# Latent stage of a hybrid encoder layer: weighing in two halves, queries and folds at the weighing, rests of latent tiles on GpSimd

## The reference

```python
qh = jnp.einsum('bsr,re->bse', _rmsnorm(cq, mla_q_norm_g), w_q_up).reshape(B, S, H_MLA, MLA_NOPE + MLA_ROPE)
...
s = (jnp.einsum('bqhd,bkhd->bhqk', qnb, kn, preferred_element_type=jnp.float32)
     + jnp.einsum('bqhr,bkr->bhqk', qrb, kr, preferred_element_type=jnp.float32)) * scale
p = jax.nn.softmax(s, axis=-1)
return jnp.einsum('bhqk,bkhd->bqhd', p.astype(v.dtype), v)
```

## Time and profile before

| | us |
|---|---|
| median of 3 runs | 1691.41 (1690.59 to 1698.48) |
| the profiled execution | 1694.89, its span 1693.4 |
| latent stage in the span | about 505 to 793 |
| TensorE busy over the span | 1494.2 (88%) |
| VectorE, ScalarE, GpSimd busy | 1095.5, 879.8, 252.6 |

### The profile page before, as it was taken

How to read it: one execution, slowest core, us unless ns; L and a number is a source line. 1 busy time by engine, 2 the same in 40 slices (tenths; PEclk the granted TensorE clock), 3 DMA queues, 4 the chain that set the end, 5 groups by cost and what they waited for, 6 DMA issues and landing times.

```text
span 1693.4 us, 21659 instructions
## 1 busy us (share of the span) xinstructions
PE 1494.2 (88%) x7474; PEld 1246.0 (74%) x7474; DVE 1095.5 (65%) x1617; ACT 879.8 (52%) x1144; POOL 252.6 (15%) x226
## 2 busy tenths in 40 slices
PE   6999999999967798995799974999999999999970
PEld 5888788888856677774588863778878778877860
DVE  5655655434336766662355554989888888888864
ACT  6433433333324545542334351867777777777744
POOL 0000111111110000000012212323213212321210
PEclk9999999999987999997799976999999999999995
DMA  7122412122113012002643353999999999999958
GB/s 240 64 92 92 154 57 88 57 64 75 44 36 96 14 38 75 26 13 80 239 150 125 133 192 108 341 379 381 388 381 387 369 381 383 376 382 385 386 151 306
DMA packets 80212, 327.07 MB, mean 193 GB/s; under 512 B 13762, under 2 KB 24002, under 8 KB 55570
## 3 DMA queue, kind: packets, MB, share of 16 engines
q1 hardware_dynamic: 63426, 278.82, 43.8%
q0 software_dynamic: 16720, 47.40, 9.5%
HBM read 281.71 MB, written 53.90 MB: 198 GB/s over the span
## 4 chain that ended last, share of the span: by engine, by line
DMA 20%; PE 13%; DVE 9%; issue 6%; ACT 4%; SPq 1%; POOL 0%; ACTq 0%; DVEq 0%; POOLq 0%
DMA plain<-in_w_down 17%; DVE split L1642 7%; PE acc L96 4%; PE acc L97 4%; PE acc L98 4%; PE acc L1828 1%; DMA plain<-s_h_rows,plain 1%; ACT split L1636 1%; ACT split L2253 1%; ACT plain L2286 1%; DMA plain<-s_w_fold 1%; POOL s_x_mid L2107 0%; ACT plain L1866 0%; PE acc L1821 0%; DMA s_table<-plain 0%
## 5 line engine op out<-in xcount | busy, mean ns | idle before, releaser
L1642 DVE TENSOR_TENSOR split<-plain,split 128x2048 fp32r<-128x2048 f32 x192 | 428.4, 2285 | 6.8 <-ACT split L1636 6.8
L96 PE MATMUL acc<-split 128*128 128x512 f32 x960 | 389.9, 406 | 36.4 <-DVE split L1891 24.3
L1636 ACT CAST split<-plain 128x2048 fp32r<-128x2048 f32 x192 | 365.3, 1916 | 98.1 <-DMA plain<-in_w_up 66.9
L98 PE MATMUL acc<-split 128*128 128x512 f32 x960 | 381.5, 397 | 0.0
L97 PE MATMUL acc<-split 128*128 128x512 f32 x960 | 381.4, 397 | 0.0
L96 PEld LDWEIGHTS acc<-split 128*128 128x128 f32 x960 | 184.8, 192 | 78.8 <-issue 30.3
L98 PEld LDWEIGHTS acc<-split 128*128 128x128 f32 x960 | 184.7, 192 | 40.4
L97 PEld LDWEIGHTS acc<-split 128*128 128x128 f32 x960 | 185.5, 193 | 36.4
L96 PE MATMUL a_p<-a_w_hi,a_xT_hi 128*128 128x512 f32 (+1 forms) x480 | 194.4, 405 | 4.1 <-DVE a_w_lo L688 4.1
L98 PE MATMUL a_p<-a_w_hi,a_xT_lo 128*128 128x512 f32 (+1 forms) x480 | 186.7, 389 | 0.0
L97 PE MATMUL a_p<-a_w_lo,a_xT_hi 128*128 128x512 f32 (+1 forms) x480 | 186.2, 388 | 0.0
(11 more groups left out here) (322 smaller groups left out, 2376.0 us busy)
## 6 DMA issues: line engine op xcount, KB each, us to landing
plain<-in_w_gate SPq DMA_DIRECT2D x64, 1024.0 KB
plain<-in_w_up SPq DMA_DIRECT2D x64, 1024.0 KB
plain<-in_w_down SPq DMA_DIRECT2D x64, 1024.0 KB, 10.8
a_x_sb<-in_x SPq DMA_DIRECT2D x24, 512.0 KB, 4.0
s_mid<-a_kv SPq DMA_DIRECT2D x12, 512.0 KB, 2.9
a_kv<-s_mid SPq DMA_DIRECT2D x12, 512.0 KB, 3.6
plain<-s_mixT SPq DMA_DIRECT2D x12, 512.0 KB, 6.0
plain<-in_x SPq DMA_DIRECT2D x12, 512.0 KB, 3.7
```

The source lines that it names most:

```text
L96: pe.matmul(out, st_hi, mv_hi, start=first, stop=False)
L98: return pe.matmul(out, st_lo, mv_hi, start=False, stop=last)
L1636: eng.copy(self.w_hi[:, j // 2, cols], self.raw[:, j // 2, cols]).then_inc(self.s_whi[j], 1)
L1642: eng.tensor_tensor(self.w_lo[:, j // 2, cols], self.raw[:, j // 2, cols], self.w_hi[:, j // 2, cols].bitcast(F32), ALU.subtract).then_inc ...
```

## The change

The three instructions of VectorE's `split_tile` move to a new GpSimd block, for all twelve tiles in order. weigh becomes weigh(g, part) with four key tiles a part; for the long sequence TensorE issues, at a fourth unit: scores(u+2), queries, weigh part 0, transposes of bank 0, fold, weigh part 1, transposes of bank 1. Queries (6) to (11) stand at units 20 to 40, folds at 16, 20, 24 and so on to 44, values at 12 to 15, split_out at 14, 22, 30, 38. take_hi of bank 0 waits only for part 0, and comes ahead of take_out. SP's order follows.

```diff
+        weighed = [sum(2 if s else 1 for s, _, _ in groups[:g]) for g in range(NG_ + 1)]
...
-            for g in range(4):
-                keep_out(g)
+            keep_out(0)
+            keep_out(1)
             for h in range(2):
                 load_out(h)
...
+            keep_out(2)
+            keep_out(3)
+            for h in range(HM):
+                keep_out(2 * h + 4)
+                keep_fold(h)
+                if h < 2:
+                    load_out(h + 2)
+                if h < 3:
+                    keep_out(2 * h + 5)
+            keep_out(NG_ - 1)
...
+        @block.gpsimd
+        def _(pool):
+            for t in range(TILES):
+                pool.wait_ge(s_chi, t + 1)
+                cols = slice(t * P, (t + 1) * P)
+                x3 = stage[t % 3].rearrange("p (k i) -> p k i", k=4)
+                nc.gpsimd.tensor_tensor(cq_lo[:, :, cols], x3[:, 0:2, :], cq_hi[:, :, cols].bitcast(F32),
+                                        ALU.subtract)
+                nc.gpsimd.tensor_tensor(key_lo[:, 0, cols], x3[:, 2, :], key_hi[:, 0, cols].bitcast(F32),
+                                        ALU.subtract)
+                nc.gpsimd.tensor_tensor(key_lo[0:DR, 1, cols], x3[0:DR, 3, :], key_hi[0:DR, 1, cols].bitcast(F32),
+                                        ALU.subtract).then_inc(s_clo, 1)
...
-                elif g == 6:
-                    pe.wait_ge(s_vlo, 3)
-                elif g in (7, 10, 11):
-                    pe.wait_ge(s_qlo, g)
-                elif g in (8, 9):
-                    pe.wait_ge(s_fev, 2 * g - 10)
+                elif g >= 6:
+                    pe.wait_ge(s_fev, g - 5)
...
+                if h == 0 and c == 0:
+                    pe.wait_ge(s_vlo, 3)
+                elif h == 3 and c == 1:
+                    pe.wait_ge(s_fev, 7)
+                else:
+                    pe.wait_ge(s_qlo, 2 * h + c + 6)
...
-                for k in range(tiles):
+                for k in range(4 * part, 4 * part + 4):
                     ins = three_passes(pe, po[:], v_hi[:, first + k, :], v_lo[:, first + k, :],
                                        pT3_hi[:, k, :], pT3_lo[:, k, :], k == 0, k == tiles - 1)
                 ins.then_inc(s_o, 1)
...
+            def aside(u):
+                if u % 4 == 0 and 20 <= u <= 40:
                     queries(u // 4 + 1)
+                elif u % 4 == 1 and 21 <= u <= 41:
+                    fold((u - 17) // 8, (u - 17) // 4 % 2)
+                elif u == 16:
+                    fold(0, 0)
+                elif u == 44:
+                    fold(3, 1)
...
                     scores(u + 2)
+                if u % 4 == 0:
+                    aside(u)
                 if u >= 4 and u % 4 == 0:
-                    weigh(u // 4 - 1)
-                transposes(u)
+                    weigh(u // 4 - 1, 0)
+                transposes(u, slice(0, 1))
+                if u > 4 * HM and u % 4 == 0:
+                    aside(u + 1)
+                    weigh(u // 4 - 1, 1)
+                transposes(u, slice(1, 2))
                 prepare(u)
-            weigh(NG_ - 1)
+            for part in range(2):
+                weigh(NG_ - 1, part)
...
                     if g:
-                        act.wait_ge(s_o, g)
+                        act.wait_ge(s_o, weighed[g] - (1 if g > HM and i == 0 else 0))
...
                     expo(u + 1)
+                if u % 4 == 0:
+                    aside(u)
+                take_hi(u, slice(0, 1))
+                if u > 4 * HM and u % 4 == 0:
+                    aside(u + 1)
                 if u >= 4 and u % 4 == 0:
                     take_out(u // 4 - 1)
-                take_hi(u)
+                take_hi(u, slice(1, 2))
                 prepare(u)
```

More of the change, by code:

```diff
@@ L1174, in scores, with transposes @@
                 ins.then_inc(s_s, 1)
-            def transposes(u):
+            def transposes(u, part):
                 pe.wait_ge(s_pn, u + 1)
-                for i, c in enumerate(banks(u)):
+                for i, c in list(enumerate(banks(u)))[part]:
                     if bank_free(u, i):
@@ L1186, in transposes, with weigh @@
                     ins.then_inc(s_pt, 1)
-            def weigh(g):
+            def weigh(g, part):
                 s, h, b = groups[g]
@@ L1210, in prepare @@
                     queries(u - 6)
[L1211 to L1217, removed]
-                    queries(u // 4 + 1)
+                elif 12 <= u < 16:
+                    values(u - 10)
+            def aside(u):
+                if u % 4 == 0 and 20 <= u <= 40:
+                    queries(u // 4 + 1)
+                elif u % 4 == 1 and 21 <= u <= 41:
[4 more added lines that the diff above has]
+                    fold(3, 1)
             pe.wait_ge(s_wlo, 1)
@@ L1310, in expo, with take_hi @@
                                      accum_out=total[:, one]).then_inc(s_exp, 1)
-            def take_hi(u):
+            def take_hi(u, part):
                 g, j = u // 4, u % 4
-                for i, c in enumerate(banks(u)):
+                for i, c in list(enumerate(banks(u)))[part]:
                     act.wait_ge(s_pt, done[u] + i + 1)
                     if g:
-                        act.wait_ge(s_o, g)
+                        act.wait_ge(s_o, weighed[g] - (1 if g > HM and i == 0 else 0))
                     nc.scalar.copy(pT3_hi[:, 4 * i:4 * i + 4, j * P:(j + 1) * P],
@@ L1322, in take_out @@
             def take_out(g):
-                act.wait_ge(s_o, g + 1)
+                act.wait_ge(s_o, weighed[g + 1])
                 if g >= 2:
@@ L1349, in prepare, with aside @@
                     take_queries(u - 6)
-                elif u in (14, 16):
-                    take_values(u // 2 - 6)
-                elif u in (18, 19):
-                    take_queries(u - 12)
-                elif 20 <= u < 31 and (u - 20) % 3 < 2:
-                    take_fold((u - 20) // 3, (u - 20) % 3)
-                elif u in (28, 32, 36, 40):
-                    take_queries(u // 4 + 1)
-                if u in (19, 22, 25, 28):
-                    split_out((u - 19) // 3)
+                elif u in (12, 14):
+                    take_values(u // 2 - 5)
+                if u in (14, 22, 30, 38):
+                    split_out(u // 8 - 1)
+            def aside(u):
+                if u % 4 == 0 and 20 <= u <= 40:
+                    take_queries(u // 4 + 1)
+                elif u % 4 == 1 and 21 <= u <= 41:
+                    take_fold((u - 17) // 8, (u - 17) // 4 % 2)
+                elif u == 16:
+                    take_fold(0, 0)
+                elif u == 44:
+                    take_fold(3, 1)
             nc.scalar.copy(w_hi[:, 0:W_VT], absorb[:]).then_inc(s_whi, 1)
@@ L1480, in prepare @@
             def prepare(u):
[L1481 to L1483 removed]
+                if u == 1:
                     rotate(2)
@@ L1503, in prepare @@
                     take_queries(u - 6)
-                elif u in (15, 17):
-                    take_values(u // 2 - 6)
-                elif u in (18, 19):
-                    take_queries(u - 12)
-                elif u in (28, 32, 36, 40):
+                elif u in (13, 15):
+                    take_values(u // 2 - 5)
+                elif u % 4 == 0 and 20 <= u <= 40:
                     take_queries(u // 4 + 1)
-                if u in (19, 22, 25, 28):
-                    split_out((u - 19) // 3)
+                if u in (14, 22, 30, 38):
+                    split_out(u // 8 - 1)
             nc.vector.memset(key_lo[DR:P, 1, :].bitcast(F32), 0.0).then_inc(s_zero, 1)
@@ L1537, in _ @@
             rot_lo(1)
-            for t in range(4, 8):
-                split_tile(t)
             peak(0)
```

38 lines of the change are left out of this document (removed).

## The result

The changed kernel takes 1684.8 us (median of 20 runs) where the kernel before takes 1695.6 in the same 20 rounds: 0.9947 of it, 95% interval 0.9936 to 0.9958, so 9.0 us less by the ratio (7.1 to 10.9 by its interval; the two medians lie 10.8 apart). The forecast was 9.1 less. The profiled execution has a span of 1681.3 us against 1693.4. Of these 12.1 us, 2.1 were already there when the latent stage began (its first matmul starts at 506.83 instead of 508.93, before any changed line runs), the stage itself is 8.3 us shorter, and 1.7 lie in the experts behind it. The change touches neither end piece; I count the 8.3. A second profiled execution of the changed kernel has a stage 7.8 us shorter than before's (272.2 us from its first matmul to the last take_out, where before has 280.0).

A forecast was written before the change was run, and what follows sets the result against it. TensorE sets the pace in the latent stage, its idle time spent waiting for VectorE. Middle -9.1, units 0 to 16 -1.5, entry +1.5, end 0 give -9.1 us off the median 1691.4: 1682.3 us, range 1675 to 1689.

The forecast's parts named there:

- Middle: Units 16 to 44, 607.5 to 768.7 us: waste falls from 18.2 to 9.1 us, so -9.1.
- rival (a): Remaining stalls: the clock falls after each of three (+3.3) and GpSimd at its upper end (+2.0): 1687.6 us; chance 0.17.
- 19.7: Sign in the last groups: take_out intervals go from 21.0 us to 19.7.
- Queries ahead: Middle: queries issued before the weighing, so VectorE no longer waits for it; steady group from 21.0 to 19.7 us.
- Rival (d): Middle: halves and queries do nothing, groups stay at 21.0 us, only better spread counts, -4.5: 1686.9 us; chance 0.13.
- Units 0 to 16: 542 to 607.5 us: tiles' rests leaving VectorE save 2.6, split_out at unit 14 costs 1.1; -1.5 us.
- 1.1 earlier than 575.10: Sign for the start of weigh(1): 1.1 us earlier than 575.10.
- Entry: 505 to 542 us: GpSimd takes 1.6 us a tile against VectorE's 0.83, counted twice: +1.5 us (0.9 to 3.5).
- End: 768.7 to 789 us: unchanged, waits of 1.99 and 1.40 and 5.1 us lost to the clock remain; 0.
- Rival (b): The clock stays up in the middle (-1.65) and at the end (-5.1): 1675.5 us; chance 0.15.
- Rival (c): Before values(0) and rotary(5): GpSimd holds up tiles, deciding from 5 us a tile; at 6, 1694.6 us; chance 0.07.
- its stall is not cured: split_out in the middle: the same wait expected in units 23, 31 and 39, 2.1 + 0.15 each, 6.75 us in all.

The follow-up runs named there:

- the kernel at 1670.9 us: The changed kernel with split_out of heads 1 to 3 moved into the weighings of units 20, 28, 36 and head 0 into unit 12's: 1670.9 us, 0.9851.

## Why the prediction was right

The total was right, to 0.1 us by the ratio, and that closeness is luck: the interval of the measurement is 3.8 us wide, the profiled stage is 8.3 us shorter, and the parts of the sum were off by +2.9 (middle), +1.1 (units 0 to 16), -2.4 (entry) and -0.8 us (end), which nearly cancel. The time itself, forecast as 1682.3, came out as 1684.8, because the kernel before takes 1695.6 over 20 rounds and not the 1691.4 of its first three. All from after's profile, relative to the start of the stage, its parts cut at the ends of weigh(3) and weigh(10):

- **Middle, -9.1 predicted, besides 1.6 us of work moved out of it, so -10.7: -7.8 measured** (161.1 to 153.3). The three stalls came where and as large as forecast (2.15, 2.12, 2.12 for 2.1), and nowhere else; with their restarts they cost 7.1 us for 6.75. The failing step is the clock: "Of three such waits I take one to be followed: 1.65". All three were, 3.3 us more; in the second measurement two. The first half of rival (a) came true, and its end of the range, 5.0, was the measured value. The work was sized too high by about 1: a group takes 20.30 where the sum's terms give 19.7 + 0.69 + 0.1 = 20.5. The sign "19.7" in the text was a slip of another kind: it left out the fold which now stands in each group. The kernel with queries alone moved has groups without a fold, 19.5.
- **Queries ahead: right** in mechanism (7.55 to 0.74 us, "under 1") and in place. Rival (d) is refuted for the queries and confirmed for the halves, which I had costed at nothing plus 0.1 a group; 0.1 was measured.
- **Folds, SP's order, weighing's waits at nothing: right.** TensorE waits for nothing in the middle but the three stalls, and the table of waits names neither a fold nor a DMA.
- **Units 0 to 16, -1.5 predicted, plus 1.6 us of moved work, so +0.1: +1.2 measured** (65.2 to 66.4, from unit 0's transposes). The stall at unit 15 was sized right (1.25 for 1.1 of TensorE). The saving was not. Up to weigh(0) 1.0 of 1.5 us was saved; weigh(0) to weigh(1) was to shrink by 1.1 (2.6 less 1.5) and shrank by 0.35, 17.97 to 17.62. In the second execution, as in nine of ten with GpSimd's rests, it grew by 1.2 instead, to 19.2, with a fall of the clock that the sum had no term for. The waits before both weighings are as before (1.69 and 1.49 against 1.70 and 1.50), as forecast; why the rest of the saving didn't come isn't shown. One part is contention, shown below: 0.3 us of VectorE once. In absolute time weigh(1) is 4.4 us earlier; of that 2.1 comes from before the stage, 0.9 from the entry and 1.4 from the units, so the sign "1.1 earlier than 575.10" was badly chosen: an absolute time collects everything ahead of it.
- **Entry, +1.5 predicted: -0.9 measured**, up to unit 0's transposes. GpSimd's part was sized right per tile (1.5 for 1.6 us) and too high on the path, 0.77 for 1.5 in this pair of profiles (9.33 against 8.56 us; before's own entry took 9.32 in another profile): the sum counted it twice, for tile 0 through the ring and for tile 3, and no more than one of the two shows. The rest goes with the clock, 0.78 of full speed over 505 to 545 us instead of 0.68 in before, which is chance between executions: the changed kernel's second one has 0.70, and all fourteen have 0.65 to 0.79.
- **End, 0 predicted: -0.8 measured**, 19.35 for 20.11 us, with waits of 1.99, 0.48 and 1.40 and the same 0.66 over 15 us as in the earlier trace rows; the middle one of the waits was 0.96.
- **Rival (b)** did not happen in this kernel; its first half is what the kernel with `split_out` at the weighing shows: with no stall no fall in the middle. **Rival (c)** is refuted: GpSimd's tile is three times below the 5 us from which it decides.

What the prediction saw as given, "its stall is not cured", was the larger prize: three stalls of 2.5 us and the falls behind them, 7 and up to 5 us, more than the whole change brought, and curable by a move of two calls.

## What to carry to other kernels

Where the bounding engine alternates between pieces with slack for its partner (here a weighing) and pieces without, put every extra step of the partner, and the work that feeds it, into the slack; in the traces this was worth 4 to 8 us for the queries and 10 to 12 for `split_out`, while dividing the slack piece itself brought nothing. Count a stall of about 2 us on TensorE at its length plus the 1.65 us of clock that followed 19 of 23 of them here, and if nothing real can fill it, unused matmuls can. Compare traces of parts of a stage by intervals, not by absolute times, and with the clock's falls taken off.

## What the runs showed of the hardware

- **One wait of about 2.1 us can cost the clock of TensorE.** Over the seven profiled executions with waits of 2.1 to 2.7 us in the middle the level fell to 1.2 GHz for some 3.3 us after 19 of 23: with stalls at units 23, 31 and 39 after three of three (in three executions) or two of three (in two), in before after two of four, and in before with its queries ahead after four of four. The identical waits at the end were followed by a fall in eleven traces of twelve, and in that of the kernel at 1670.9 us by none until the last weighing was done. With nine matmuls in each of the same waits it never fell. Which of two equal waits is followed by a fall stays open. The length of one wait doesn't settle it either: in unit 6 the kernels with GpSimd's rests wait 1.22 and, right behind it, 0.46 us, and nine of ten executions have a fall there, while those with VectorE's rests wait 1.82 us in one piece at the same place and none of four has one.
- **GpSimd beside VectorE.** A tile's instructions take 0.72, 0.45 and 0.45 us alone. At 545 us, while VectorE works on two SBUF operands, both are slower: 0.90 for 0.45 on GpSimd, and 1.01 for 0.69 on VectorE. The one call of 1.01 is in all ten profiled executions with GpSimd's rests and in none of the four without. It isn't always both: at 529.8 us GpSimd's 128x256 takes 1.04 for 0.72 beside another VectorE instruction, which keeps its 0.68. The same VectorE instruction, over all six of its calls, in before (nanoseconds, min, median, max) and the slow one in after beside GpSimd's:

```profile
L1442 DVE TENSOR_TENSOR c_rot<-absorb x6: 691/692/693, 523.7 to 573.2; 128x512 f32<-128x512 f32 x6
```

```profile
544.65 1.01 DVE L1459 TENSOR_TENSOR c_rot<-absorb 128x512 f32<-128x512 f32 x1
...
545.07 0.90 POOL L1073 TENSOR_TENSOR c_key_lo<-c_late,c_key_hi 128x128 fp32r<-128x128 f32 x1
```

The Trainium skill ("GPSIMD Engine Reference", section "Specifications") says that the two engines share their SBUF interfaces and names instructions of VectorE with two SBUF inputs among those that contend; the trace agrees, with these durations. So work that is moved to an idle GpSimd isn't always free for VectorE.
